# A two-layer hybrid decoder step on one core: three program blocks merged into one, with both layers written out

## The chip, the core and the metric

The kernel runs on one core of a Trainium2 chip. The metric is the device time of one execution in microseconds; the times below are the medians of several runs. A core has five engines that run side by side, each with its own stream of instructions: TensorE (PE, matrix products into PSUM), VectorE (DVE), ScalarE (ACT), GpSimd (POOL) and SyncE (SP), which here only issues transfers. They wait for each other by semaphores. A *block* of the program holds one stream for each engine. At the end of a block all engines meet at a barrier.

## What is computed

Two layers of a decoder on 512 prompt tokens and 8 sample tokens, width 1024, all in float32. The reference, cut to what matters here:

```python
def layer(x, pos, attn_fn, ctx_b, ctx_c, ctx_d, h0, p):
    u = rms_norm(x, p['g_pre_mix'])
    (q, k, v, qi, ki, wi, bx, gb, gc, glu, zg, xbc, dt) = jnp.split(u @ p['w_in'], cuts, axis=-1)
    ...                                   # sparse attention, two convolutions, a chunked state-space scan
    mix = jnp.concatenate([y_a, y_b, y_c, y_d], axis=-1) @ p['w_out']
    x = x + rms_norm(mix, p['g_post_mix'])
    hf = rms_norm(x, p['g_pre_ffn'])
    f = (jax.nn.silu(hf @ p['ffn_gate']) * (hf @ p['ffn_up'])) @ p['ffn_down']
    x = x + rms_norm(f, p['g_post_ffn'])
    return x, (k, v, ki, new_b, new_c, new_d, h_new.astype(x.dtype))

def rms_norm(x, g):
    xf = x.astype(jnp.float32)
    y = xf * lax.rsqrt(jnp.mean(xf * xf, axis=-1, keepdims=True) + RMS_EPS)
    return (y * g.astype(jnp.float32)).astype(x.dtype)
```

The outputs are the new activations of all tokens, and per layer the keys, values and states.

## The kernel before

**Data.** The activations `x` lie in SBUF with features on the partitions: 8 chunks `k` of 128 features by 520 tokens. Each float32 product is made of three: both operands are split into an *upper part* (ScalarE casts it, `*_hi`) and a *lower part* (value minus upper part, `*_lo`), and TensorE adds upper by upper, upper by lower and lower by upper. The lower part of a weight is made by GpSimd (lines 2474 and 2480) or VectorE (line 2120), that of an activation by VectorE (line 1704).

**Blocks.** There are three. The *prologue* (lines 351 to 412) loads the constants, the prompt (`x_rows`), and 24 small rows of parameters, turns `x` on TensorE (line 381), copies it out of PSUM (VectorE, line 408), squares it (ScalarE, line 400) and sums the squares over the features (TensorE, `sum_tokens`, line 335). The *layer* stands once, in a loop in hardware over both layers (line 554); weights are addressed by the loop's register. At its end come a barrier, the clearing of all the layer's semaphores, a barrier and the jump back. The *output* block turns `x` back (TensorE, line 2570), tile by tile of 128 tokens, copies it (VectorE, line 2579), and SP stores each tile of 128x1024 when both of its halves are there (line 2586).

**A layer's head.** SP issues seven transfers for the first three *slabs* of `w_in`, which give the outputs with tokens on the partitions: slab 0 in two pieces (`tw_raw`, and two small transfers for the `dt` columns into the same pieces), slab 1 in one, slab 2 in two. Then it stores `x` (`x_store`) and loads states and scalars. ScalarE takes the root of the mean square (`root_of`, line 1233), VectorE the reciprocal (line 1692), and TensorE spreads it over the partitions into PSUM (line 666). VectorE then scales the chunks (line 1700, one operand in SBUF, one in PSUM), ScalarE casts each (`u_hi`, line 1248), and VectorE subtracts (`m_lo`, line 1704); lower part k-2 follows scaling k. Between the casts of the chunks ScalarE casts the pieces of slab 0 (line 1241), ahead of chunks 1 and 3, and slab 1 after the last chunk; GpSimd makes their lower parts `tw_lo` (line 2480). TensorE's products with slab 0 (lines 742 to 744) wait for `tw_lo` and `m_lo`, chunk by chunk. After the first tile of slab 1 TensorE *turns* the indexer's queries and keys (line 710), which VectorE has rotated (`rope`, lines 1719 to 1760) behind them. The sparse attention and all else follow from there.

**A layer's end.** The last product with `ffn_down` (line 687) is squared and copied (ScalarE, lines 1661 and 1663), summed, rooted and spread as above. VectorE's `add_normed` scales each chunk (line 2228) and adds it to `x` (line 2232, two operands in SBUF). ScalarE squares the new chunk (line 1675) and TensorE sums (line 335), for the next layer's root; in the last layer this is done as well.

Of the kernel before, what the change touches and what calls it, by code (L numbers as in the profile page):

```python
# [26 lines left out]
ACT = mybir.ActivationFunctionType  # L27
# [90 lines left out]
def hybrid_decoder(nc, d, out):  # L118
# [16 lines left out]
    sems = []  # L135

    def sem(name):
        sems.append(ctx.enter_context(nc.semaphore(name)))
        return sems[-1]

    with ctx:
# [208 lines left out]
        with nc.Block() as block:  # L350
            @block.sync
            def _(sp):
                sp.dma_start(x8, d["x_sample"].rearrange("b s f -> (b s) f")).then_inc(sample_in, 16)
                sp.dma_start(cst[:, :], d["constants"]).then_inc(const_in, 16)
                for t in range(QT):
                    sp.dma_start(x_rows[:, t, :], d["x_prompt"][0, t * P:(t + 1) * P, :]).then_inc(rows_in, 16)
                sp.dma_start(pages[:, :], d["page_table"].rearrange("(o b) g -> o (b g)", o=1)).then_inc(pages_in, 16)
                for l in range(DEPTH):
                    for rows, tile in zip((ROWS_A, ROWS_B), rows_of[l]):
                        at = 0  # L360
                        for name, n in rows:
                            src = d[name][l:l + 1]
                            src = src.rearrange("o (c p) -> (o c) p", p=P) if src.ndim == 2 else \
                                src.rearrange("o t (c p) -> (o t c) p", p=P)
                            sp.dma_start(tile[at:at + n, :], src).then_inc(params_in, 16)
                            at += n
                sp.wait_ge(pages_in, 16)

            @block.tensor
            def _(pe):  # L370
                pe.wait_ge(const_in, 16)
                pe.wait_ge(sample_in, 16)
                for c in range(KC):
                    last = pe.transpose(bank(7)[:, c * NS:(c + 1) * NS], x8[:, c * P:(c + 1) * P], ident[0:NS, 0:NS])
                last.then_inc(x8_turned, 1)
                pe.wait_ge(rows_in, 16 * QT)
                for c in range(KC):
                    if c == 7:
                        pe.wait_ge(x_copied, 1)
                    for t in range(QT):  # L380
# [2238 lines left out]
```

## Time and profile before

| | us |
|---|---|
| median of 3 runs | 1496.69 |
| lowest and highest | 1494.46 and 1497.63 |
| the profiled execution | 1494.14 |
| its span, first to last instruction | 1492.6 |
| TensorE, products: busy | 1370.0 (92%), 11078 products |
| VectorE busy | 1029.2 (69%) |
| ScalarE busy | 654.5 (44%) |
| GpSimd busy | 195.8 (13%) |
| granted clock of TensorE, mean | 0.962 |

The span has three parts: the prologue to about 20 us, the two layers of about 732 us each, and the output from 1479.6 on. A row of the timeline gives the start and the length in us, the engine, the line of the kernel, the operation with what it writes and reads, how many instructions of the kind are merged into the row, and in brackets how long the engine was idle before and what released it. PEld is TensorE's load of weights, and SPq are transfers that SP issues. Rows of one engine may overlap by a tenth, since its instructions are pipelined.

### The profile page before, as it was taken

Reading aid. Unit: us, or ns where it says so; the run is one execution under the profiler, and the core shown is the slowest. Engines: PE = TensorE matmul, PEld = TensorE weight load, DVE = VectorE, ACT = ScalarE, POOL = GpSimd, SP = SyncE. Lnnn points to the kernel's source line nnn. Section 1 sums busy time; section 2 is a strip of 40 time slices with the busy share of each in tenths; the row PEclk is TensorE's granted clock in tenths of the full one; section 3 lists DMA queues with packets and bytes.
Section 4 is the critical chain, followed back from the end, with each engine's and each line's share of the span. In section 5 each row is a group of like instructions: output and inputs, shape, how many; then the busy total and the mean of one; then the engine's idle time right before and its main releaser. Section 6 shows DMA issues by size and latency. Waiting matters only on the chain. (4 is left out here: it accounts for less than half of the span.)

```text
span 1492.6 us, 29816 instructions
## 1 busy us (share of the span) xinstructions
PE 1370.0 (92%) x11078; PEld 1265.0 (85%) x11078; DVE 1029.2 (69%) x2147; ACT 654.5 (44%) x1199; POOL 195.8 (13%) x136
## 2 busy tenths in 40 slices
PE   4999978987999999999769998799979999999995
PEld 4889854787999999999657997648979999999994
DVE  5489998744899999322446898987269999972225
ACT  3443225443556666222344422445354566652222
POOL 1325312011000000010041442121100000000100
PEclk8999989998999999999879999999989999999997
DMA  6444231131523333432064333212322333343221
GB/s 222 137 119 115 72 100 60 62 99 43 156 72 110 101 99 103 155 96 89 9 209 141 110 85 89 68 63 84 96 92 86 100 101 110 100 142 112 88 67 58
DMA packets 223312, 149.96 MB, mean 100 GB/s; under 512 B 13579, under 2 KB 218739, under 8 KB 222167
## 3 DMA queue, kind: packets, MB, share of 16 engines
q1 hardware_dynamic: 220582, 141.09, 31.7%
q0 software_dynamic: 2624, 7.48, 1.3%
q8 instruction: 65, 1.06, 0.3%
q14 instruction: 41, 0.33, 0.1%
HBM read 128.92 MB, written 16.03 MB: 97 GB/s over the span
## 5 line engine op out<-in xcount | busy, mean ns | idle before, releaser
L1152 PE MATMUL PS<-b_hi,a_hi 128*128 128x260 f32 x1008 | 285.8, 284 | 3.0 <-DVE last_lo L2315 2.2
L1152 PE MATMUL PS<-b_lo,a_hi 128*128 128x260 f32 x1008 | 283.9, 282 | 0.0
L2120 DVE TENSOR_TENSOR w_lo<-ring,w_hi 128x640 fp32r<-128x640 f32 (+2 forms) x88 | 87.5, 994 | 242.3 <-ACT w_hi L1383 241.9
L1152 PEld LDWEIGHTS PS<-b_hi,a_hi 128*128 128x128 f32 x1008 | 189.6, 188 | 4.5 <-DVE last_lo L2315 2.7
L1152 PEld LDWEIGHTS PS<-b_lo,a_hi 128*128 128x128 f32 x1008 | 190.1, 189 | 0.0
L1383 ACT CAST w_hi<-ring 128x1024 fp32r<-128x1024 f32 (+2 forms) x92 | 80.1, 871 | 237.1 <-PE PS L687 237.1
L788 PE MATMUL PS<-u_hi,w_hi 128*128 128x260 f32 x576 | 122.1, 293 | 15.5 <-ACT hid L1325 15.5
L687 PE MATMUL PS<-hid_hi,w_lo 128*128 128x260 f32 x656 | 132.2, 283 | 0.0
L687 PE MATMUL PS<-hid_hi,w_hi 128*128 128x260 f32 x656 | 132.0, 282 | 0.0
L687 PE MATMUL PS<-hid_lo,w_hi 128*128 128x260 f32 x656 | 131.7, 282 | 0.0
L1152 PE MATMUL PS<-b_hi,s_lo 128*128 128x260 f32 x432 | 121.9, 282 | 0.0
L1152 PE MATMUL PS<-b_hi,raw_lo 128*128 128x260 f32 x432 | 121.9, 282 | 0.0
L2474 POOL TENSOR_TENSOR w_lo<-ring,w_hi 128x1024 fp32r<-128x1024 f32 x36 | 86.3, 2397 | 268.8 <-ACT w_hi L1271 268.8
L788 PE MATMUL PS<-m_lo,w_hi 128*128 128x260 f32 x576 | 120.7, 289 | 0.0
L788 PE MATMUL PS<-u_hi,w_lo 128*128 128x260 f32 x576 | 120.1, 289 | 0.0
L788 PEld LDWEIGHTS PS<-u_hi,w_hi 128*128 128x128 f32 x576 | 90.9, 192 | 22.3 <-ACT hid L1325 16.9
L2544 POOL TENSOR_TENSOR side<-side 128x520 f32<-128x520 f32 x12 | 15.7, 1310 | 709.9 <-ACT u L1663 709.9
L687 PEld LDWEIGHTS PS<-hid_hi,w_lo 128*128 128x128 f32 x656 | 101.0, 188 | 0.0
L687 PEld LDWEIGHTS PS<-hid_hi,w_hi 128*128 128x128 f32 x656 | 101.0, 188 | 0.0
L687 PEld LDWEIGHTS PS<-hid_lo,w_hi 128*128 128x128 f32 x656 | 101.0, 188 | 0.0
L1555 ACT CAST a_hi<-ring 128x512 fp32r<-128x512 f32 x144 | 89.5, 622 | 16.5 <-PE PS L1152 16.2
L788 PEld LDWEIGHTS PS<-m_lo,w_hi 128*128 128x128 f32 x576 | 91.1, 192 | 2.9 <-issue 2.9
(396 smaller groups left out, 3351.7 us busy)
## 6 DMA issues: line engine op xcount, KB each, us to landing
ring<-in_ffn_gate SPq DMA_DIRECT2D x44, 512.0 KB, 3.6
ring<-in_ffn_up SPq DMA_DIRECT2D x44, 512.0 KB, 3.7
ring<-in_w_in SPq DMA_DIRECT2D x36, 512.0 KB, 3.7
ring<-in_ffn_down SPq DMA_DIRECT2D x32, 384.0 KB, 3.4
ring<-in_ffn_down SPq DMA_DIRECT2D x32, 320.0 KB, 3.1
x_store<-x SPq DMA_DIRECT2D x4, 2080.0 KB
x<-x_store SPq DMA_DIRECT2D x4, 2080.0 KB, 7.8
ring<-in_w_out SPq DMA_DIRECT2D x16, 512.0 KB, 4.1
```

The lines of the kernel that those rows point to most:

```text
L687: ins = pe.matmul(to[:, h, :], w[:, k - base, :], a[k][:, h * HALF:(h + 1) * HALF], start=(begin and w is whi and a is a_hi), stop=(end an ...
L788: last = pe.matmul(bank(tile_bank(i) + h)[:, 0:HALF], w[i % 2][:, k, :], t[:, h * HALF:(h + 1) * HALF], start=(k == 0 and a == 0), stop=(k ...
L1152: ins = pe.matmul(bank(ACC[up][to])[:, 0:HALF], w[:, k, :], b[:, k, :], start=(start and k == 0 and w is whi and b is bhi), stop=(k == KC ...
L1383: act.copy(w_hi[part % 2][:, 0:n, :], raw[part % 4][:, 0:n, :]).then_inc(part_hi, 1)
L1555: act.copy(a_hi[hi_block(q, at)][:, :, :], source if q not in (S1, S2, S4) else source[:, :, :])\
L2120: dve.tensor_tensor(w_lo[part % 2][:, 0:n, :], raw[part % 4][:, 0:n, :], w_hi[part % 2][:, 0:n, :].bitcast(F32), ALU.subtract).then_inc(pa ...
L2474: pool.tensor_tensor(w_lo[f % 2][:, :, :], raw[(f + 2) % 4], w_hi[f % 2][:, :, :].bitcast(F32), ALU.subtract).then_inc(tile_lo, 1)
L2544: pool.tensor_tensor(squares[:, 0, :], squares[:, 0, :], squares[:, m, :], ALU.add).then_inc(added, 1)
```

## The change

The three blocks become one, and the barriers and the clearing of semaphores between them go. The loop over the layers is written out when the program is built: `layer` is a number, and the code of a layer stands twice. A semaphore is not cleared any more; each has a count of what one layer adds to it (`sem(name, in_layer)`), and `past(layer, s, value)` adds the earlier layers' part to what is waited for. All waits inside a layer are rewritten so; of these the diff shows two. Waits and addresses inside the remaining inner loops still go by registers.

With the fences gone, five things move:

- SP asks for layer 0's slabs behind the prologue's small loads, and for layer 1's slabs when the last product of layer 0 is done (`down_part`). `x_store` waits for `x`.
- ScalarE casts the two pieces of slab 0 ahead of all chunks: in layer 0 right behind the root, in layer 1 already at the end of layer 0, ahead of squares 2 and 4. Their lower parts stay on GpSimd.
- The last layer's squares and their sum go.
- TensorE turns the output chunk by chunk of features: after each chunk's add the four tiles' piece, in two halves of four chunks. The small tile of the samples is turned at the end of each half.
- The copies out of PSUM go from VectorE to ScalarE, and SP stores each half of a tile (128x512) as it is copied.

```diff
-        sems = []
-        def sem(name):
-            sems.append(ctx.enter_context(nc.semaphore(name)))
-            return sems[-1]
+        per_layer = {}
+        def sem(name, in_layer=0):
+            s = ctx.enter_context(nc.semaphore(name))
+            per_layer[s.num] = in_layer
+            return s
...
+        def past(l, s, value):
+            return s, value + l * per_layer[s.num]
...
-        with nc.Fori(0, DEPTH) as layer:
-            with nc.Block() as block:
-                @block.sync
-                def _(sp):
+                for layer in range(DEPTH):
                     l = layer
...
+                    if layer:
+                        sp.wait_ge(*past(layer, down_part, 0))
                     for (a, b, _, _), t in zip(tok_pieces[0], slab_raw[0]):
...
+                    if layer:
+                        sp.wait_ge(*past(layer, x_updated, 0))
+                    else:
+                        sp.wait_ge(x_copied, KC + 1)
                     sp.dma_start(x_store, x[:, :, :].rearrange("p k t -> p (k t)")).then_inc(x_kept, 16)
...
+                for n, (t, q) in enumerate(Y_ORDER):
+                    sp.wait_ge(*past(DEPTH, y_copied, n + 1))
+                    to = y_prompt[0, t * P:(t + 1) * P, :] if t < QT else y_sample.rearrange("b s f -> (b s) f")
+                    sp.dma_start(to[:, q * 512:(q + 1) * 512], y_rows[0:P if t < QT else NS, t, q * 512:(q + 1) * 512])\
+                      .then_inc(y_stored, 16)
...
-                    sum_squares(pair(0), squares_ready, KC)
+                    if layer + 1 < DEPTH:
+                        sum_squares(pair(0), squares_ready, KC)
+                for q in range(2):
+                    for c in range(4):
+                        pe.wait_ge(*past(DEPTH, x_updated, 4 * q + c + 1 - KC))
+                        for t in range(QT):
+                            if q == 1 and c == 0 and t >= 2:
+                                pe.wait_ge(*past(DEPTH, y_copied, t - 1))
+                            last = pe.transpose(bank(Y_BANK[t, q])[:, c * P:(c + 1) * P], x[:, 4 * q + c, t * P:(t + 1) * P], ident)
...
                     root_of(0, pair(0), 1.0 / D_MODEL, 0)
+                    if layer == 0:
+                        slab_upper(0, 0)
+                        slab_upper(0, 1)
                     for k in range(KC):
-                        if k in (1, 3):
-                            slab_upper(0, k // 2)
-                        act.wait_ge(m_scaled_ready, k + 1)
+                        act.wait_ge(*past(layer, m_scaled_ready, k + 1))
...
-                    for k in range(KC):
-                        act.wait_ge(x_updated, KC + k + 1)
+                    for k in range(KC if layer + 1 < DEPTH else 0):
+                        if k in (2, 4):
+                            slab_upper(0, k // 2 - 1, layer + 1)
+                        act.wait_ge(*past(layer, x_updated, KC + k + 1))
                         act.activation(squares[:, k, :], x[:, k, :], ACT.Square).then_inc(squares_ready, 1)
+                for n, (t, q) in enumerate(Y_ORDER):
+                    m = P if t < QT else NS
+                    act.wait_ge(*past(DEPTH, y_turned, n + 1))
+                    act.copy(y_rows[0:m, t, 512 * q:512 * (q + 1)], bank(Y_BANK[t, q])[0:m, :]).then_inc(y_copied, 1)
...
-            nc.all_engine_barrier()
-            nc.gpsimd.sem_clear(range(sems[first_layer_sem].num, sems[last_layer_sem - 1].num + 1))
-            nc.all_engine_barrier()
```

How the instructions stand, at three places. A row gives the line, the operation, what it writes and reads, the size, and the semaphores that it waits for.

SP between the prologue and layer 0, before. `arena<-in_dconv_b` is the last small load, `tw_raw` are the slabs' pieces:

```order
L365 DMA arena<-in_dconv_b 6x128
L350 UNCONDITIONAL_BRANCH [waits pages_in]
L554 UNCONDITIONAL_BRANCH [waits barrier_Pool_Activation_PE_DVE_SP_release]
L557 UNCONDITIONAL_BRANCH
L565 ISA
L565 DMA tw_raw_75<-in_w_in 128x4x4
```

And now, without a fence between them:

```order
L514 DMA arena<-in_dconv_b 6x128
L526 DMA tw_raw_75<-in_w_in 128x4x4 [waits pages_in]
L526 DMA tw_raw_76<-in_w_in 128x4x4
L529 DMA tw_raw_75<-in_w_in 128x4x296
L529 DMA tw_raw_76<-in_w_in 128x4x296
L529 DMA tw_raw_79<-in_w_in 128x8x384
L529 DMA tw_raw_84<-in_w_in 128x3x384
L529 DMA tw_raw_85<-in_w_in 128x5x384
L534 DMA x_store<-x 128x4160 [waits x_copied]
```

The slabs' transfers moved up to the small loads, in the same order, and `x_store` waits for `x`.

ScalarE at the end of a layer, before. `side` and `u` take the last product, `arena<-x` are the eight squares:

```order
L1661 ACTIVATE side<-PS 128x520 [waits down_part]
L1663 COPY u<-PS 128x520
L1233 ACT_TABLE_LOAD
L1233 ACTIVATE root<-PS,cst 128x130 [waits sums_ready]
L1675 ACTIVATE arena<-x 128x520 [waits x_updated] x8
L555 UNCONDITIONAL_BRANCH
L554 REGISTER_ALU [waits barrier_Pool_Activation_PE_DVE_SP_release]
L554 COMPARE_AND_BRANCH
```

And now, from the end of layer 0 into layer 1:

```order
L1248 ACT_TABLE_LOAD
L1248 ACTIVATE root<-PS,cst 128x130 [waits sums_ready]
L1693 ACTIVATE arena<-x 128x520 [waits x_updated] x2
L1256 CAST tw_hi_71<-tw_raw_75 128x1200 [waits slab_in00,dt_w_in]
L1693 ACTIVATE arena<-x 128x520 [waits x_updated] x2
L1256 CAST tw_hi_72<-tw_raw_76 128x1200 [waits slab_in01,dt_w_in]
L1693 ACTIVATE arena<-x 128x520 [waits x_updated] x4
L1248 ACTIVATE root<-PS,cst 128x130 [waits sums_ready]
L1264 CAST u_hi<-arena 128x520 [waits m_scaled_ready] x8
L1256 CAST tw_hi_77<-tw_raw_79 128x3072 [waits slab_in10]
```

The two casts of slab 0 stand between the squares, and the next layer's root follows the last square with no table load. The chunks' eight casts stand in one piece, and slab 1's cast is behind them as before.

TensorE at the end of the program, before. `arena` are the squares and `cst,x` the transposes; `turned_ready` counts the copies of the output:

```order
L335 MATMUL PS<-arena,cst 32x130 [waits squares_ready]
L335 MATMUL PS<-arena,cst 32x130 x3
L555 UNCONDITIONAL_BRANCH
L554 REGISTER_ALU [waits barrier_Pool_Activation_PE_DVE_SP_release]
L554 COMPARE_AND_BRANCH
L2561 UNCONDITIONAL_BRANCH
L2570 MATMUL PS<-cst,x 128x128 x32
L2570 MATMUL PS<-cst,x 8x128 [waits turned_ready]
L2570 MATMUL PS<-cst,x 8x128 x3
```

And now, the last two chunks of the first half, and the first of the second:

```order
L1229 MATMUL PS<-cst,x 128x128 [waits x_updated]
L1229 MATMUL PS<-cst,x 128x128 x3
L1229 MATMUL PS<-cst,x 128x128 [waits x_updated]
L1229 MATMUL PS<-cst,x 128x128 x3
L1234 MATMUL PS<-cst,x 8x128 [waits turned_ready]
L1234 MATMUL PS<-cst,x 8x128 x3
L1229 MATMUL PS<-cst,x 128x128 [waits x_updated]
L1229 MATMUL PS<-cst,x 128x128
L1229 MATMUL PS<-cst,x 128x128 [waits turned_ready] x2
```

The transposes now stand right behind the last spread; each group of four waits for one add of `x`, and only the second half's first chunk and the small tiles wait for copies too.

## Rows read from the trace of the kernel before

**Rows 1.** The page, costliest groups: busy, mean | idle before, what ended it

```profile
L1152 PE MATMUL PS<-b_hi,a_hi 128*128 128x260 f32 x1008 | 285.8, 284 | 3.0 <-DVE last_lo L2315 2.2
```

**Rows 2.** Timeline, prologue to layer 0: start, length, engine, line, operation, count [idle before]

```profile
12.24 0.30 SPq L365 DMA_DIRECT2D arena<-in_dconv_b  x1
...
17.07 1.83 ACT L400 ACTIVATE u<-x 128x520 f32<-128x520 f32 x3 [0.20 <-DVE x L408]
...
17.79 1.98 PE L335 MATMUL PS<-u,cst 128*32 128x130 f32 x64
...
20.80 1.28 ACT L1233 ACT_TABLE_LOAD   x1 [1.90 <-PEq L414]
...
20.95 1.02 SPq L565 DMA_DIRECT2D tw_raw<-in_w_in  x2
...
22.09 0.37 ACT L1233 ACTIVATE root<-PS,cst 128x130 f32<-128x130 f32 x1
...
25.65 2.09 DVE L1700 SCALAR_TENSOR_TENSOR arena<-x,par,PS 128x520 f32<-128x520 f32 x3 [2.19 <-PE PS L666]
```

**Rows 3.** Timeline, head of layer 0

```profile
26.97 1.19 ACT L1241 CAST tw_hi<-tw_raw 128x1200 fp32r<-128x1200 f32 x1
...
28.24 5.90 POOL L2480 TENSOR_TENSOR tw_lo<-tw_raw,tw_hi 128x1200 fp32r<-128x1200 f32 x2 [27.53 <-ACT tw_hi L1241]
...
28.93 2.59 DVE L1704 TENSOR_TENSOR m_lo<-arena,u_hi 128x520 fp32r<-128x520 f32 x1
...
31.11 0.59 PE L742 MATMUL PS<-tw_hi,u_hi 128*128 128x300 f32 x1 [5.50 <-POOL tw_lo L2480]
...
38.48 2.77 ACT L1241 CAST tw_hi<-tw_raw 128x3072 fp32r<-128x3072 f32 x1
...
41.32 13.93 POOL L2480 TENSOR_TENSOR tw_lo<-tw_raw,tw_hi 128x3072 fp32r<-128x3072 f32 x3 [7.18 <-ACT tw_hi L1241]
...
57.20 1.53 PE L710 MATMUL PS<-cst,arena 128*128 128x128 f32 x12 [0.99 <-DVE arena L1760]
...
57.89 1.56 ACT L1265 COPY arena<-PS 128x512 f32<-128x512 f32 x3 [1.10 <-PE PS L710]
```

**Rows 4.** Timeline, end of layer 0 to the turn in layer 1

```profile
730.27 0.41 PE L687 MATMUL PS<-hid_hi,w_lo 128*128 128x260 f32 x2
...
739.15 0.64 ACT L1675 ACTIVATE arena<-x 128x520 f32<-128x520 f32 x1 [0.64 <-DVE x L2232]
...
740.97 0.69 DVE L2232 TENSOR_TENSOR x<-x,u 128x520 f32<-128x520 f32 x1
...
744.80 1.31 DVE L2232 TENSOR_TENSOR x<-x,u 128x520 f32<-128x520 f32 x2
...
746.22 1.27 PE L335 MATMUL PS<-arena,cst 128*32 128x130 f32 x16 [0.62 <-ACT arena L1675]
...
752.96 1.94 SPq L565 DMA_DIRECT2D tw_raw<-in_w_in  x2
...
757.93 2.09 DVE L1700 SCALAR_TENSOR_TENSOR arena<-x,par,PS 128x520 f32<-128x520 f32 x3 [2.19 <-PE PS L666]
...
789.48 1.53 PE L710 MATMUL PS<-cst,arena 128*128 128x128 f32 x12 [1.77 <-DVE arena L1760]
```

**Rows 5.** Stretches: us, busy time and count of each engine, granted clock, DMA

```profile
733.00:736.00 3.00, 1.16 (x8) 0.97 (x8) 1.16 (x2) 0.47 (x2) 0.00 (x0) 1.00 0.00 0
...
738.00:747.50 9.50, 5.23 (x64) 1.61 (x64) 8.11 (x13) 4.94 (x8) 0.00 (x0) 0.50 0.01 2
...
755.00:758.00 3.00, 2.10 (x8) 1.80 (x8) 0.81 (x2) 0.00 (x0) 0.00 (x0) 0.50 0.67 152
```

**Rows 6.** Timeline, end of the run

```profile
1476.88 1.30 DVE L2232 TENSOR_TENSOR x<-x,u 128x520 f32<-128x520 f32 x2
...
1481.58 7.35 PE L2570 MATMUL PS<-cst,x 128*128 128x128 f32 x40 [2.02 <-PEq L2555]
...
1486.99 3.14 DVE L2579 COPY arena<-PS 128x512 f32<-128x512 f32 x5 [0.16 <-PE PS L2570]
```

More of the change, by code:

```diff
@@ L1230, in root_of, with _ @@
+            @block.scalar
+            def _(act):
+                for k in range(KC):
+                    act.wait_ge(x_copied, k + 2)
+                    act.activation(x_squares[:, k, :], x[:, k, :], ACT.Square).then_inc(x_squared, 1)
+                for layer in range(DEPTH):
                     def root_of(n, sums, scale, eps):
-                        if n:
-                            act.wait_ge(sums_ready, n)
+                        if n or layer:
+                            act.wait_ge(*past(layer, sums_ready, n))
+                        else:
+                            act.wait_ge(x_summed, 1)
@@ L1378, in upper @@
                     def upper(part, free, value, turn, n=KC):
-                        act.wait_ge(raw_in[part % 4], turn)
-                        act.wait_ge(free, value)
+                        act.wait_ge(*past(layer, raw_in[part % 4], turn))
+                        act.wait_ge(*past(layer, free, value))
                         act.copy(w_hi[part % 2][:, 0:n, :], raw[part % 4][:, 0:n, :]).then_inc(part_hi, 1)
@@ L2458, in _ @@
                         lower(p, 4 * KC - 8 + DN0 + p + 1, DOWN_PARTS[p % 4][1])
-                    dve.wait_ge(down_ready, 2 * KC + 4)
+                    dve.wait_ge(*past(layer, down_ready, 2 * KC + 4))
                     add_normed(3, u, "g_post_ffn")
-                    dve.wait_ge(x_updated, 2 * KC)
-                @block.gpsimd
-                def _(pool):
+                    dve.wait_ge(*past(layer, x_updated, 2 * KC))
+            @block.gpsimd
+            def _(pool):
+                for layer in range(DEPTH):
                     l = layer
@@ L2477, in slab_lower @@
                     def slab_lower(s, i):
-                        pool.wait_ge(slab_hi, sum(len(p) for p in tok_pieces[:s]) + i + 1)
+                        pool.wait_ge(*past(layer, slab_hi, sum(len(p) for p in tok_pieces[:s]) + i + 1))
                         pool.tensor_tensor(tw_lo[s][i][:, :, :], slab_raw[s][i][:, :, :], tw_hi[s][i][:, :, :].bitcast(F32),
```

878 lines of the change are left out of this document (424 added, 454 removed).

## The prediction

> **What bounds the kernel now.** I read the page first, then the timeline at the three places where one block of the program ends and the next begins, because that is where the diff acts. In the page's groups the long stretches belong to TensorE: the largest matmul group has 3.0 us of idle time in 285.8 us of work [rows 1]. The diff leaves these stretches alone. At the three fences TensorE waits instead, and a chain that hops between engines sets the time. At the first one the last square sum ends at 19.77, and ScalarE's root starts at 22.09, behind a barrier and a table load of 1.28 us [rows 2]. At the one between the layers the sum ends at 747.49, and the first weight transfer is issued at 752.96 [rows 4]. At the last one ScalarE and TensorE finish a sum of squares that nobody reads, and the transposes for the output start at 1481.58 [rows 6].
>
> The reader should also see who holds whom in a layer's head. GpSimd's two lower parts take 5.90 us together, and during them VectorE's lower parts of the activations take 2.59 us where the same size takes 0.69 (0.69 is the add's row) [rows 3, 4]. TensorE starts at 31.11, when the first lower part is there. A second chain runs beside it: the last activation, then the cast of slab 1 at 38.48, GpSimd's three lower parts to 55.25, VectorE's rope step behind them, and TensorE's turn at 57.20, which waits 0.99 us for it [rows 3]. So the head has two paths that end within 1 us of each other.
>
> **The change, part by part.** All sums are against the profiled execution: span 1492.6, run 1494.14.
>
> *Prologue to layer 0.* The weights' seven transfers are issued once the small loads are out, near 12.7 instead of 20.95 (the last small load is issued at 12.24) [rows 2]. In the run before, the first cast was not held up at 26.97, 6.0 us after the first issue [rows 2, 3], so they are there by 18.7. ScalarE's squares end at 18.90 [rows 2]; the table load still stands ahead of the root, so the root runs at about 20.2, 1.85 earlier. The root to the first scaled chunk took 3.56 us [rows 2], with the spread at the slow clock: 2.10 us of TensorE at 0.50 against 1.16 at 1.00 [rows 5]. Here TensorE has rested only 1.9 us, so I take the fast one: 20.2 + 3.56 - 0.94, some 23.0 after rounding up (bounds 22.8 and 23.8). That is 2.6 earlier than 25.65. The casts follow the root at once (2 x 1.19), so GpSimd works from 21.9 to 27.8 (5.90) [rows 3]. VectorE's first lower part comes up at 25.1, three scalings later (2.09), and is held to about 28.2. TensorE starts there instead of at 31.11: 2.9 us. Only one lower part is held now instead of two, 2.5 us lost instead of 3.8, so the second chain gains 2.6 + 1.3 = 3.9. At the turn the first path gains 2.9 and the 0.99 of waiting that goes, also 3.9. **Layer 0: 3.9 us** (bounds 2.9, if only TensorE's start counts, and 5.6, if VectorE slips in between GpSimd's two operations).
>
> *Layer 0 to layer 1.* The barriers, the clearing of semaphores and the jump back go, and ScalarE's table load with them, since the root's function set is already in place. If that were all, the root would come at 747.6, 0.1 after the sum. But the first slab's casts are now placed between the squares, after the second and the fourth. Their weights can be asked for from 730.68 on, when the last product ends [rows 4]; by the 6.0 us above they are there by 737. The first cast starts at 739.8, right behind the second square, and the second at 742.3. ScalarE has the room: a square takes 0.64 in a step of 1.28 [rows 4]. GpSimd then runs from 741.0 to 746.9, and VectorE's adds of two SBUF operands, 0.69 each, fall under it. The add at 740.97 gets in, just; the next waits to 744.0 and the one after to 746.9, and each ends 0.4 later, as the held rows did. The last two follow behind two scalings, and the last add ends near 749.3 instead of 746.11 [rows 4]: 3.2 us back. (If GpSimd wins the tie at 740.97, it is 3.9.) From the last add to the end of the sum is 1.38 (746.11 to 747.49), so the root runs at 750.7, and 3.56 later, at 754.3, the first chunk is scaled; TensorE's clock is at 0.50 in such a stretch of thin sums [rows 5], so I take the slow spread. That is 3.6 before 757.93. From there on no lower part is held: 3.8 more for the second chain, 7.4 in all. The first path would be 6.4 earlier and loses its 1.77 of waiting at 789.48 [rows 4], 8.2, so the second chain decides. **Layer 1: 7.4 us** (bounds 5.5, with a further add held, and 10.6, with none).
>
> The Trainium skill ("SBUF — State Buffer", section "SBUF: two separate sides") says that GpSimd and a VectorE operation with two SBUF inputs take one port pair as an exclusive lock for the whole instruction. By that rule the scalings, which read one operand from PSUM, go free, and the adds do not; the row of 2.59 us agrees [rows 3].
>
> *The end.* The squares and the sum of the last layer go. TensorE's 32 large transposes, 7.35 us with the small ones [rows 6], are done chunk by chunk as the adds end. An add comes each 1.28 us and four transposes take at most 0.92 (7.35 over eight chunks), so all but the last chunk is hidden. After the last add, 1478.18 [rows 6], the first tile's bank is complete at about 1478.75. The copies move to ScalarE: 0.52 each for 128x512 from PSUM [rows 3], four of them and the samples' small one, to about 1481.4. Before, the last copy ended at 1490.13 and the span 2.47 later [rows 6]. I keep the 2.47, since the last large transfer is half the size. **End: 8.8 us** (bounds 7.5, if each copy takes 0.69 as VectorE's did and the queue adds to the tail, and 9.3).
>
> *With one answer each:* constants instead of registers in waits, and fixed addresses in transfers, touch sequencers that wait anyway: nothing. x's store in layer 1 stands behind the weights on SP's queue and waits for the last add; what is behind it (the states, the caches) stood behind the weights before too, is issued earlier now, and is wanted only at the turn or later. GpSimd's waits for the stores at a layer's end now stand ahead of its first lower part, and those stores are long out.
>
> Sum: 3.9 + 7.4 + 8.8 = 20.1. The span would be 1472.5, the profiled run 1474.0, and against the median, which is 2.55 above the profiled run, **1476.6**.
>
> **The rivals.**
> *A: the adds are not held.* For it: none of the trace's adds ever met GpSimd, so their rows all read 0.69. Against: the lower parts have the same operand form and were held. Layer 1 gains 10.6 instead of 7.4: 1473.4.
> *B: smaller gains all along.* The transfers of 4.3 MB now run beside the prologue's loads, so the casts come late and layer 0 gains 2; two further waits at the layers' fence leave 4.7; the end gives 7.5. Together 14.2: 1482.5. For it: no row shows these transfers beside other loads. Against: they have 7.9 us until the first cast (12.7 to 20.6) where 6.0 was enough, and the pieces needed first are first in the queue.
> *C: it does nothing.* The head's gain is used up by a later wait on VectorE's top-k chain, and the end waits on the output transfers, 2 MB. Against: both paths that leave the head shift together, and the output transfers kept up before. Within 3 us of 1496.7.
> *D: slower, by fetching code.* With the layers written out the program is twice as long, and the loops that remain sit at other addresses. A taken jump may have to fetch its target: the fence with the jump back took 5.5 us (747.49 to 752.96) [rows 4], the last one without it left TensorE idle for 2.0 [rows 6], so 3.5 us for a jump is the bound. TensorE jumps back 16 times in the program's inner loops (6 and 2 in each layer): 56 us, 1532.6. It decides from 6 such jumps on. Against: the same loops with the same bodies show no gap now [rows 1].
> The Trainium skill ("Runtime: NRT & Kernel Launch", section "Instruction fetch mechanics") says that a taken branch to a target outside the current window stalls for a fetch. No row separates this from the barrier; it speaks for a gain at the fence as much as for D.
>
> **How the numbers follow.** Forecast 0.60, its own range 1474.5 to 1480; A 0.13; B 0.17; C 0.03; D 0.04; the rest, between B and C, 0.03. The range 1470.5 to 1482 takes in the forecast and its bounds (some 24 to 16 us of gain, and 1 us for the medians' scatter), A, and a third of B: about 0.8. A measurement of this kernel can tell about 0.2%, 3 us, from no change. Faster by more: 0.93, within: 0.03, slower: 0.04.
>
> **What the profile after would show.** TensorE's first slab product at about 28.2; the cast of slab 1 near 34.6; no table load before the second root. At the layers' fence one or two adds of 2 to 3 us beside GpSimd, the last one ending near 749.3 less the 3.9 of layer 0, and then the root within 1.5 us. In layer 1 all lower parts at 0.69. At the end the transposes between the adds, and some 5.7 us from the last add to the end of the span. Wrong would be: adds all at 0.69 (A), casts waiting on transfers (B), or gaps in TensorE at a loop's first product (D).

## The result, and the profile after

The changed kernel takes 1477.53 us (median of 4 runs, 1474.74 to 1478.38), the kernel before 1495.58 on the same chip (4 runs, 1490.53 to 1497.63). The ratio is 0.988, with a 95% interval of 0.985 to 0.991: 18.05 us or 1.2% faster. In a later series of five runs it was 1474.72 against 1493.17, ratio 0.988 again (0.986 to 0.990). The profiled execution took 1478.38 with a span of 1476.4 us; before it was 1494.14 and 1492.6.

The sum can be read at a few marks that both programs have. The first is the end of the prologue's last square sum. Then come TensorE's transposes behind VectorE's rope step in each layer (the "turn"), the first add of the expert output to x in each layer, and the start of the row with the last two adds. All columns are profiled executions; "again" is a second one, of the later series.

| stretch | before | after | again | gain of after | of again |
|---|---|---|---|---|---|
| start to the last square sum | 19.77 | 19.26 | 20.81 | 0.5 | -1.0 |
| sum to the turn of layer 0 (head) | 37.43 | 33.44 | 33.74 | **4.0** | **3.7** |
| turn to the first add (nothing changed in it) | 679.94 | 681.15 | 678.69 | -1.2 | 1.25 |
| first add to the turn of layer 1 (fence and head) | 52.34 | 45.84 | 45.73 | **6.5** | **6.6** |
| turn to the last two adds (nothing changed in it) | 687.40 | 688.76 | 688.78 | -1.4 | -1.4 |
| last two adds to the end | 15.72 | 7.95 | 7.95 | **7.8** | **7.8** |
| span | 1492.6 | 1476.4 | 1475.7 | 16.2 | 16.9 |

The three edited places give 18.3 and 18.1 us, which is what the medians say. What the profiled spans lack of it was lost in the start and in stretches that the edit does not touch.

The timeline of after, from the prologue into layer 0, answers [rows 2, 3]. As there, a row gives start and length in us, engine, line, operation, what it writes and reads, the count, and in brackets the idle time before and its releaser:

```profile
12.07 0.95 SPq L526 DMA_DIRECT2D tw_raw<-in_w_in  x2
...
18.62 1.28 ACT L1248 ACT_TABLE_LOAD   x1
...
19.91 0.37 ACT L1248 ACTIVATE root<-PS,cst 128x130 f32<-128x130 f32 x1
...
20.18 2.27 ACT L1256 CAST tw_hi<-tw_raw 128x1200 fp32r<-128x1200 f32 x2
21.44 5.40 POOL L2513 TENSOR_TENSOR tw_lo<-tw_raw,tw_hi 128x1200 fp32r<-128x1200 f32 x2 [20.98 <-ACT tw_hi L1256]
23.14 2.09 DVE L1732 SCALAR_TENSOR_TENSOR arena<-x,par,PS 128x520 f32<-128x520 f32 x3 [1.86 <-PE PS L661]
...
25.14 2.25 DVE L1736 TENSOR_TENSOR m_lo<-arena,u_hi 128x520 fp32r<-128x520 f32 x1
...
27.45 0.62 PE L737 MATMUL PS<-tw_hi,u_hi 128*128 128x300 f32 x1 [4.35 <-DVE m_lo L1736]
...
33.74 2.76 ACT L1256 CAST tw_hi<-tw_raw 128x3072 fp32r<-128x3072 f32 x1
...
36.58 13.83 POOL L2513 TENSOR_TENSOR tw_lo<-tw_raw,tw_hi 128x3072 fp32r<-128x3072 f32 x3 [9.74 <-ACT tw_hi L1256]
...
52.70 1.53 PE L705 MATMUL PS<-cst,arena 128*128 128x128 f32 x12 [0.61 <-DVE arena L1792]
```

The casts run straight behind the root, without waiting for a transfer. One lower part of VectorE meets GpSimd and takes 2.25 us, the others 0.69. TensorE starts at 27.45 instead of 31.11, and its wait at the turn is 0.61 instead of 0.99.

The same program between the layers, answering [rows 4]:

```profile
733.85 0.70 DVE L2264 TENSOR_TENSOR x<-x,u 128x520 f32<-128x520 f32 x1
...
736.39 1.18 ACT L1256 CAST tw_hi<-tw_raw 128x1200 fp32r<-128x1200 f32 x1
...
737.74 6.36 POOL L2513 TENSOR_TENSOR tw_lo<-tw_raw,tw_hi 128x1200 fp32r<-128x1200 f32 x2 [23.20 <-ACT tw_hi L1256]
...
738.96 2.56 DVE L2264 TENSOR_TENSOR x<-x,u 128x520 f32<-128x520 f32 x1
...
742.11 2.55 DVE L2264 TENSOR_TENSOR x<-x,u 128x520 f32<-128x520 f32 x1
...
745.25 1.30 DVE L2264 TENSOR_TENSOR x<-x,u 128x520 f32<-128x520 f32 x2
...
747.99 0.37 ACT L1248 ACTIVATE root<-PS,cst 128x130 f32<-128x130 f32 x1 [0.78 <-PE PS L337]
...
751.56 2.09 DVE L1732 SCALAR_TENSOR_TENSOR arena<-x,par,PS 128x520 f32<-128x520 f32 x3 [2.20 <-PE PS L661]
...
779.69 1.53 PE L705 MATMUL PS<-cst,arena 128*128 128x128 f32 x12 [0.61 <-DVE arena L1792]
```

The root follows the last add by 1.44 us and has no table load ahead of it. But two of the eight adds take 2.56 and 2.55 us beside GpSimd's first pair of lower parts. The first add in the timeline of before:

```profile
737.14 0.69 DVE L2232 TENSOR_TENSOR x<-x,u 128x520 f32<-128x520 f32 x1
```

Now it comes 3.29 us earlier, and the last one ends 0.44 later (746.55 against 746.11 [rows 4]): 3.73 us given back.

The end, answering [rows 6]:

```profile
1465.37 1.12 PE L1229 MATMUL PS<-cst,x 128*128 128x128 f32 x4 [0.16 <-DVE x L2264]
1465.89 2.05 ACT L1697 COPY arena<-PS 128x512 f32<-128x512 f32 x4 [9.02 <-PE PS L1229]
...
1467.50 1.02 PE L1234 MATMUL PS<-cst,x 128*8 128x128 f32 x4 [1.01 <-ACT arena L1697]
...
1468.32 3.62 PE L1229 MATMUL PS<-cst,x 128*128 128x128 f32 x16
1468.45 1.31 DVE L2264 TENSOR_TENSOR x<-x,u 128x520 f32<-128x520 f32 x2
...
1471.33 2.48 ACT L1697 COPY arena<-PS 128x512 f32<-128x512 f32 x5 [2.20 <-PE PS L1229]
```

The transposes now stand between the adds, four of them (1.12 us) per chunk. From the end of the last add (1469.76) to the end of the span are 6.6 us; before they were 14.4.

### The profile page after: what moved, and what is told of

Its sections match the earlier page's. It is cut to its first block, busy times and chain, and to the rows that moved or that the text cites. A ratio compares the mean times of both kernels' runs of the same rounds, so it can differ in the third digit from the quotient of the medians.

```text
span 1476.4 us, 29324 instructions
## 1 busy us (share of the span) xinstructions
PE 1370.9 (93%) x11014; PEld 1269.0 (86%) x11014; DVE 1018.2 (69%) x2137; ACT 653.4 (44%) x1200; POOL 195.5 (13%) x136
## 4 chain that ended last, share of the span: by engine, by line
PE 82%; DVE 12%; ACT 3%; issue 2%; DMA 1%; SPq 0%; ACTq 0%; DVEq 0%
PE PS L682 30%; PE PS L1147 24%; PE PS L783 12%; PE PS L754 2%; PE PS L910 2%; PE PS L755 2%; PE PS L756 2%; PE PS L661 1%; DVE x L2264 1%; PE PS L698 1%; PE PS L737 1%; PE PS L738 1%; PE PS L739 1%; PE PS L337 1%; DVE arena L1751 1%
## 5 line engine op out<-in xcount | busy, mean ns | idle before, releaser
L783 PEld LDWEIGHTS PS<-u_hi,w_hi 128*128 128x128 f32 x576 | 91.6, 194 | 22.4 <-ACT hid L1341 16.9
L1571 ACT CAST a_hi<-ring 128x512 fp32r<-128x512 f32 x144 | 89.5, 621 | 16.5 <-PE PS L1147 16.2
```

Of the source, the lines that this page charges most:

```text
L783: last = pe.matmul(bank(tile_bank(i) + h)[:, 0:HALF], w[i % 2][:, k, :], t[:, h * HALF:(h + 1) * HALF], start=(k == 0 and a == 0), stop=(k ...
L1571: act.copy(a_hi[hi_block(q, at)][:, :, :], source if q not in (S1, S2, S4) else source[:, :, :])\
```

## The experiments

Two series were run, each on one chip beside the kernel before (median 1493.51 of 7 runs in the first, 1493.17 of 8 in the second). The names in brackets are the labels of the table behind them.

**Is the give-back between the layers GpSimd holding VectorE's adds (e1)?** Layer 1's first casts move behind the second root, as layer 0 has them, so that GpSimd starts when the adds are over:

```
-                    if layer == 0:
-                        slab_upper(0, 0)
-                        slab_upper(0, 1)
+                    slab_upper(0, 0)
+                    slab_upper(0, 1)
...
-                        if k in (2, 4):
-                            slab_upper(0, k // 2 - 1, layer + 1)
```

> Edit: layer 1's two casts of slab 0 stand behind the second root, as in layer 0, and no longer between the squares; the weights are still asked for early. Theory (port lock): GpSimd is then idle under layer 0's adds, so all eight take 0.69 us and the last one ends 3.7 us sooner after the first (9.0 instead of 12.7). In layer 1 GpSimd's two operations hold one activation lower part for 2.3 us, as in layer 0 of the changed kernel, and from the first scaled chunk to the turn it takes 29.5 instead of 28.2 us. Net 2.3 us faster than the changed kernel. Rival (the early casts pay): slab 0 is then what TensorE waits for, and the head of layer 1 loses the 3.8 us that were forecast for it: as fast as the changed kernel or up to 1.5 us slower.

Timeline of this kernel, between the layers:

```profile
738.70 1.30 DVE L2261 TENSOR_TENSOR x<-x,u 128x520 f32<-128x520 f32 x2
...
741.72 2.27 ACT L1256 CAST tw_hi<-tw_raw 128x1200 fp32r<-128x1200 f32 x2
...
743.07 5.41 POOL L2510 TENSOR_TENSOR tw_lo<-tw_raw,tw_hi 128x1200 fp32r<-128x1200 f32 x2 [31.03 <-ACT tw_hi L1256]
...
747.03 2.01 DVE L1733 TENSOR_TENSOR m_lo<-arena,u_hi 128x520 fp32r<-128x520 f32 x1
```

The adds are free of delay again: from the start of the first (731.04) to the end of the last are 8.96 us, as before the change (8.97), where after has 12.70. One lower part of the activations is held in their place (2.01). From the first add to the turn are 43.57 us, 2.3 less than in after. Five profiles with after's code at this place read 45.7 to 46.4, so the difference is real and 2.2 to 2.9 in size. The adds were held by GpSimd, and casting between the squares costs more than it brings.

**What if GpSimd has no lower part there at all (e2)?** In layer 1 VectorE makes slab 0's two lower parts itself, in the gaps on both sides of its reciprocal:

```
+                        if layer:
+                            slab0_lower(0)
...
+                        if layer:
+                            slab0_lower(1)
...
-                    for s in range(N_TOK):
+                    for s in range(1 if layer else 0, N_TOK):
```

> Edit: in layer 1 VectorE makes slab 0's two lower parts, the first between the last add and the reciprocal (it is idle there for 1.85 us), the second between the reciprocal and the first scaling (idle 2.2 us); layer 0 and the casts are as in the changed kernel. Theory (port lock): the adds are free, 3.7 us sooner, and each lower part, some 1.4 us by VectorE's 1.23 us for 1024 columns, lies in a gap, so that nothing is given back: 3.7 us faster than the changed kernel at the turn of layer 1. Rival (the adds are late for another reason, such as ScalarE's casts between the squares): the adds still take 2.6 us twice, and the two lower parts change nothing or cost up to 2.8 us.

Timeline of this kernel, VectorE between the last add and the first lower part of the activations:

```profile
743.79 1.40 DVE L1729 TENSOR_TENSOR tw_lo<-tw_raw,tw_hi 128x1200 fp32r<-128x1200 f32 x1
...
745.33 0.97 DVE L1724 RECIPROCAL rstd<-root 128x130 f32<-128x130 f32 x1
746.21 1.34 DVE L1729 TENSOR_TENSOR tw_lo<-tw_raw,tw_hi 128x1200 fp32r<-128x1200 f32 x1
...
750.50 0.69 DVE L1746 TENSOR_TENSOR m_lo<-arena,u_hi 128x520 fp32r<-128x520 f32 x1
```

VectorE needs 1.40 and 1.34 us for what took GpSimd about 3 us each, and it has this time: nothing waits for it there. First add to turn 42.28, 3.6 us less than in the profile of after (3.4 to 4.2 over the five). The 3.73 us given back are regained.

**What did the fence cost, the meeting of the engines or what came with it (e4)?** The engines meet between the layers by a semaphore, and layer 1's weights are asked for and cast behind it; no jump, no clearing, no table load:

```
+                    if layer:
+                        sp.sem_inc(x8_turned, 1)
+                        sp.wait_ge(x8_turned, 6)
...
```

The same stands in each engine's program at the layer's start, and the casts stand as in e1.

> Edit: between the layers all five engines meet at a semaphore again; weights are asked for and cast behind it; no jump back, no clearing of semaphores, no table load. All else as in the changed kernel. Theory (the jump, the clearing and the table load are the price of the fence, the meeting itself costs some 0.3 us): from the end of the last sum to the issue of the first weight transfer 0.5 instead of 5.5 us, adds free (3.7 us less than the changed kernel), root at once, but the casts wait for the weights, 6 us after the issue, and two lower parts are held again; from the first scaled chunk to the turn about 32 us. So within 1.5 us of the changed kernel at the turn. Rival (the meeting itself costs, or the early request is what pays): 4 us or more slower than the changed kernel at the turn.

Timeline of this kernel, the last square sum, the first request and the root:

```profile
740.71 1.27 PE L337 MATMUL PS<-arena,cst 128*32 128x130 f32 x16 [0.62 <-ACT arena L1699]
...
741.42 0.94 SPq L529 DMA_DIRECT2D tw_raw<-in_w_in  x2
...
742.11 0.37 ACT L1257 ACTIVATE root<-PS,cst 128x130 f32<-128x130 f32 x1 [0.84 <-PE PS L337]
```

The last square sum ends at 741.98 and the root runs at 742.11; SP had issued the weights at 741.42, ahead of the sum's modelled end. In the kernel before 5.47 us lay between the sum and this issue [rows 4]. From the first add to the turn are 46.6 us, 5.8 less than before and within 0.9 of after's five profiles. So this meeting is cheap. It is also a weak one, as it let the engines go before TensorE's last products had ended; whether a block's barrier waits for them is not known. What was dear is that wait, the clearing, the jump back or the start of each engine's program anew, and this run does not tell these apart. In the changed kernel the weights' early request brings almost nothing at this place, because its gain goes into the held adds. Without that it pays: e1 and e4 both cast behind the root, and e1, which asks early and has no meeting, is 3.0 us faster to the turn (43.57 against 46.58).

**Is it the early request in layer 0 (e5)?** SP asks for the weights of layer 0 only when the first square sum is there, about where the kernel before did:

```
+                    else:
+                        sp.wait_ge(x_summed, 1)
```

> Layer 0's weights are asked for only when the first square sum is done, about where the kernel of before asked for them; everything else as in the changed kernel. Theory, that in layer 0 the earlier request carries the gain: casts from about 25.4 us instead of 20.2, the first slab product at 32 to 33 us instead of 27.45, the turn of the first slab about 5 us later than 52.7, and the time about as much longer than the changed kernel's. Rival, that the chain of root, reciprocal and scalings sets the start and the weights would be early enough anyway: the turn at most 1 us later.

Timeline of this kernel, the first cast of slab 0:

```profile
25.03 1.19 ACT L1258 CAST tw_hi<-tw_raw 128x1200 fp32r<-128x1200 f32 x1 [4.47 <-DMA tw_raw<-in_w_in]
```

The casts come at 25.03 and wait for the transfer, and from the sum to the turn are 37.15 us, against 33.44 in after and 37.43 before. So nearly the whole gain in layer 0 is the early request; without it the missing barrier is worth only 0.3 us. TensorE's first slab product came at 29.64, earlier than I expected, because VectorE's first lower part got in between GpSimd's two (1.19 us), and only the second was held in full (2.58). So the turn is 3.7 us late and not 5.

**How much of the end is the order of the output (e3)?** The blocks are merged, but the output is made as before: the square sum is kept, transposes stand behind it, VectorE copies, and each tile is sent whole.

> Edit: the output as in the kernel before (squares and sum of the last layer kept, transposes tile by tile behind them, copies by VectorE, whole rows stored), but in the same block without a fence. All else as in the changed kernel. Theory (the chunk by chunk order is worth its share, the fence 2 us): from the last add to the end of the span 12.4 us (14.4 before, less the 2.0 us fence), so 5.8 us slower than the changed kernel, which took 6.6. Rival (most of the tail was the fence, and the end is set by the transfers): 9 us or less, 2.4 us slower at most.

Timeline of this kernel, its end:

```profile
1467.49 5.77 PE L1229 MATMUL PS<-cst,x 128*128 128x128 f32 x40
1468.72 6.39 DVE L2489 COPY arena<-PS 128x512 f32<-128x512 f32 x10 [2.69 <-PE PS L1229]
```

The transposes start 0.1 us after the sum (1467.41) instead of 2.0 after it [rows 6]. From the last add (1466.03) to the end are 11.4 us: 3.0 of the 7.8 us come with the missing block border, 4.8 with the new order. The border's share is more than its 2.0 us of waiting, since the 40 transposes also took 5.77 us instead of 7.35: TensorE's granted clock was 0.50 from 1467 to 1469, 0.76 to 1471 and 1.00 behind that, and before it was 0.50 from 1481 to 1487.

**What holds the new end (e6)?** The samples' transposes shared a PSUM bank with a tile's; now that tile has a free bank, and VectorE copies two of the second halves beside ScalarE:

```
-        Y_BANK = {(0, 0): 0, (1, 0): 1, (2, 0): 2, (3, 0): 3, (4, 0): 2, (0, 1): 6, (1, 1): 7, (2, 1): 0, (3, 1): 1, (4, 1): 3}
+        Y_BANK = {(0, 0): 0, (1, 0): 1, (2, 0): 2, (3, 0): 3, (4, 0): 6, (0, 1): 7, (1, 1): 0, (2, 1): 1, (3, 1): 2, (4, 1): 3}
...
+                for t in (1, 3):
+                    dve.wait_ge(*past(DEPTH, y_turned, QT + 1 + t + 1))
+                    dve.tensor_copy(y_rows[0:P, t, 512:1024], bank(Y_BANK[t, 1])).then_inc(params_turned, 1)
```

> Only the end is changed: tile 4's first half has a bank of its own, so that its transposes wait for no copy, and the second halves of tiles 1 and 3 are copied by VectorE beside ScalarE. Theory, that the end of the changed kernel is set by the five copies of 0.5 us in a row on ScalarE and by the transposes that start 1.1 us behind the last add: last add to the end of the span 5.2 us instead of 6.64, the time 1.4 us shorter than the changed kernel's. Rival, that the last transfer's own time sets it: 6.3 to 6.6 us.

Timeline of this kernel, its end:

```profile
1464.21 1.27 PE L1232 MATMUL PS<-cst,x 128*128 128x128 f32 x8 [0.23 <-DVE x L2270]
1465.18 1.53 ACT L1703 COPY arena<-PS 128x512 f32<-128x512 f32 x3 [1.81 <-PE PS L1232]
...
1465.36 1.29 DVE L2502 COPY arena<-PS 128x512 f32<-128x512 f32 x2 [0.60 <-PE PS L1232]
```

Last add (1464.76) to the end of the span: 5.5 us instead of 6.6. The first copy of a second half starts 0.42 us behind the last add instead of 1.57; this is the whole gain, and sharing the copies brought nothing on top. (The last transposes also ran at a granted clock of 1.00 here, at 0.50 in after. For the first copy that is worth 0.1 us at most, as only one of them stands ahead of it behind the last add.) The rate of the transfers says why. First after, from 1460 to 1477 in 40 slices of 0.425 us, then this kernel, from 1455 to 1471 in slices of 0.4:

```profile
GB/s 0 0 0 0 0 0 0 0 0 0 0 0 0 0 0 0 0 260 405 410 415 390 405 222 0 0 0 0 0 0 337 405 424 400 390 414 135 0 0 0
```

```profile
GB/s 0 0 0 0 0 0 0 0 0 0 0 0 0 0 0 0 0 0 220 404 410 405 410 400 399 16 0 0 0 338 405 410 389 410 405 307 0 0 0 0
```

The second burst is near 400 GB/s in both, in after from about 1472.8 to 1475.7, in this kernel from 1466.6 to 1469.4. Each starts 0.9 us after the first copy's end, and ends 0.7 to 0.9 before the span does. A second half of 1.05 MB takes 2.6 us at that rate. So both my copies and the rival's transfer were half right: the first copy starts the end, and the stream of transfers sets its length. The median of all runs, 1474.84, does not show the 1.1 us beside 1474.72, as the scatter of single runs is larger (1471.33 to 1478.07).

**Both together (e7), and the changed kernel again (e0).** VectorE makes slab 0's lower parts in both layers, with the end of e6:

> VectorE makes slab 0's lower parts in both layers (in layer 0 the first behind the reciprocal and the second behind the last scaling), and the output copies are shared as in the kernel with the end alone changed. Theory, that GpSimd's two-operand subtractions hold VectorE's wherever they meet: against the changed kernel the head of layer 0 loses the held scaling's 1.5 us, the stretch from the first expert add of layer 0 to the turn of layer 1's first slab falls from 45.85 to 42.2 us, and the end from 6.6 to 5.2: the span 6.6 us shorter than the changed kernel's. Rival, that VectorE's own work in those gaps delays its squares and scalings as much as it saves: layer 0's head gains nothing or loses up to 1 us, and the whole is 4 to 5 us faster, nearly all of it from the fence and the end.

> The changed kernel itself once more, beside the kernel of before and the other kernels of this call, so that they can be compared on one chip. Both readings (the clock granted between 300 and 372 us and between 800 and 1140 us was chance, or it belongs to the changed kernel) are told apart here: by the first the gain at the turn of layer 0 (4.5 us) still stands to within 0.5 us at the last product of layer 0 in at least one of the two profiles of this kernel, by the second both profiles show it falling to 3.6 us.

The marks of all profiled executions, in us; the ratios are each to the kernel before in the same series (after's own: 1495.58; e1 to e4: 1493.51), and "unchanged" is a stretch that no edit touches:

| kernel | sum to turn, layer 0 | unchanged | first add to turn, layer 1 | unchanged | last add to the end | median us (runs) | ratio to before |
|---|---|---|---|---|---|---|---|
| before | 37.43 | 679.94 | 52.34 | 687.40 | 14.4 | 1493.17 (8) | |
| after | 33.44 | 681.15 | 45.84 | 688.76 | 6.6 | 1477.53 (4) | 0.988 |
| after again, e0 | 33.74 | 678.69 | 45.73 | 688.78 | 6.6 | 1474.72 (5) | 0.988 |
| e1, casts late | 33.51 | 679.10 | 43.57 | 684.59 | 6.6 | 1473.72 (4) | 0.987 |
| e2, VectorE's lower parts in layer 1 | 33.56 | 681.13 | 42.28 | 684.45 | 6.7 | 1470.36 (4) | 0.985 |
| e3, old output | 33.61 | 676.92 | 46.29 | 688.09 | 11.4 | 1481.33 (4) | 0.992 |
| e4, meeting kept | 33.67 | 677.73 | 46.58 | 688.70 | 6.7 | 1476.73 (4) | 0.988 |
| e5, asked late | 37.15 | 679.16 | 46.38 | 686.28 | 6.7 | 1478.93 (4) | 0.991 |
| e6, end | 33.62 | 676.81 | 46.44 | 686.31 | 5.5 | 1474.84 (4) | 0.988 |
| e7, VectorE's in both layers, end of e6 | 32.67 | 678.61 | 42.15 | 689.14 | 5.5 | 1468.64 (5) | 0.983 |

The last kernel beats both: 0.983 of before, with an interval of 0.981 to 0.985, and 6.1 us below the changed kernel by the medians of one series. By the marks it is 0.8 to 1.1 in layer 0, 3.6 to 3.7 in layer 1 and 1.1 at the end. In layer 0 the theory wanted 1.5, and its rival nothing or a loss. The missing part seems to have another cause. From the timelines, first e0, then e7, the spread of the reciprocals ahead of the scalings:

```profile
22.52 1.16 PE L661 MATMUL PS<-rstd,cst 128*128 128x130 f32 x8 [1.71 <-DVE rstd L1724]
```

```profile
21.66 1.84 PE L664 MATMUL PS<-rstd,cst 128*128 128x130 f32 x8 [2.12 <-DVE rstd L1730]
```

The spread takes 2.10 us at half the clock and 1.16 at the full one [rows 5]; it read 1.16 in five of the nine profiles and 1.23 to 1.84 in the others, with the same code. In e7 it took 0.68 us more than in e0; the granted clock from 21.5 to 23.6 was 0.73 and then 0.50 there, and 1.00 in e0. From the last sum to the first slab product are 6.76 us in e7 and 7.83 in e0; this 1.07 is also the gain at the turn. With the spread of e0 it would be 1.75 by my estimate; no run shows it. That the turn follows TensorE's start is new, too: in both kernels GpSimd now waits 0.75 us for slab 1's second cast, which stands behind ScalarE's copy of TensorE's products. Timeline of e7, GpSimd in layer 0:

```profile
35.43 6.80 POOL L2533 TENSOR_TENSOR tw_lo<-tw_raw,tw_hi 128x3072 fp32r<-128x3072 f32 x1 [34.97 <-ACT tw_hi L1260]
42.98 6.94 POOL L2533 TENSOR_TENSOR tw_lo<-tw_raw,tw_hi 128x1152 fp32r<-128x1152 f32 x2 [0.75 <-ACT tw_hi L1260]
```

So the two chains out of a layer's head are level, and a gain on one of them alone is soon worth nothing. The same fits the 45.7 to 46.4 that this code's stretch read in layer 1. From the first slab product to ScalarE's first copy were 14.4 to 14.5 us where it was shortest (after, e0) and 14.9 to 15.1 where GpSimd had to wait 0.6 to 0.8 (e3, e5, e6).

The columns "unchanged" show what the 2.6 us are that the profile of after lost there (1.2 and 1.4). The second profile of the changed kernel does not fall back in layer 0: it gains 1.25 us there where the first lost 1.2. The stretch takes 676.8 to 681.2 us, the other 684.5 to 689.1. Their means over the nine profiles of changed programs are 678.8 and 687.2, against 679.9 and 687.4 in the one profile of before. TensorE's clock is part of that scatter. From the views by stretches (length, then busy time and count of each engine, granted clock, DMA share, GB/s), the first row of before, the second of after, the third of e6:

```profile
300.00:372.00 72.00, 60.59 (x511) 58.20 (x508) 31.44 (x46) 29.97 (x45) 11.44 (x8) 0.93 0.22 65
```

```profile
300.00:372.00 72.00, 61.40 (x493) 59.06 (x491) 30.75 (x43) 31.47 (x47) 11.45 (x8) 0.88 0.18 54
```

```profile
300.00:372.00 72.00, 60.85 (x523) 57.72 (x525) 32.19 (x42) 32.42 (x50) 11.43 (x8) 0.93 0.18 54
```

At a mean of 0.88 TensorE is busy 61.40 us of these 72, at 0.93 it is 60.85. Which of the two comes does not follow the edit: before, e1, e3, e4, e5 and e6 show 0.93; after, e0, e2 and e7 show 0.88. It does not explain all of the scatter (e7 has 0.88 and a short stretch), and the rest I leave open.

## Why the prediction was right

The forecast was 1476.6 us and the median is 1477.53; the range and the sign held. The gain itself was put at 20.1 and is 18.05 (medians) or 18.0 to 18.3 (marks), so the sum was a tenth too large. The time came out closer than that because the kernel before also measured 1.1 us lower once its fourth run was in (1495.58 instead of 1496.69).

*Layer 0, forecast 3.9, measured 4.0 and 3.7.* The mechanism held: transfers issued at 12.07, the root at 19.91 (20.2 expected) with the casts straight behind it, first scaling at 23.14 (23.0), one lower part held, first product at 27.45 (28.2), slab 1's cast at 33.74 (34.6). The late request (e5) shows that the gain is the transfer's place in SP's queue. That the sum came out to 0.1 us is in part luck, since errors of its terms cancel. Measured from the last square sum, the first scaling is only 2.0 us earlier (3.88 behind it instead of 5.88), where I had 2.6: the root came 0.3 early, less than the 0.5 by which the prologue was shorter by chance, and the spread took 1.76 us and not 1.16, at a granted clock of 0.61 and then 0.50. The other term, forecast at 1.3, is 2.2: from the first scaling to GpSimd's work on slab 1 are 13.44 us instead of 15.67, because the held lower part took 2.25 and not 3.1. It ends with GpSimd's pair, which started 0.46 before my 21.9 and took 5.40 instead of 5.90. In e0, with the fast spread, the terms were 3.0 and 1.6, and GpSimd then waited 0.75 for a cast. TensorE's wait at the turn did not go either; it is 0.61 instead of 0.99.

*Layers' fence and head, forecast 7.4, measured 6.5 (5.9 to 6.6 over the five profiles with this code).* The mechanism was the forecast's and not rival A's: no table load, root 1.44 us behind the last add, all lower parts of the activations at 0.69, and two adds held. Even the tie went as said: with all times of the forecast 3.3 earlier, as the first add came, the first cast (739.8) lies at 736.5 and was at 736.39, and the add at 740.97 lies at 737.67, where it got in 0.06 us ahead of GpSimd. The mis-sized term is what follows: I had 3.2 us and it was 3.73. I had let GpSimd take 5.90 us, as in layer 0 before, where one operation of VectorE got in ahead of its second lower part. Here the add that got in holds GpSimd's first one as well, and the pair took 6.36, 0.46 more; both held adds wait for it.

Another 0.34 is in the rope step. Before, VectorE's first operation got in ahead of GpSimd and the second was held (timeline, VectorE in layer 0):

```profile
50.54 0.52 DVE L1719 TENSOR_TENSOR arena<-arena,cst 128x256 f32<-128x256 f32 x1 [10.61 <-ACT arena L1287]
50.98 4.41 DVE L1720 TENSOR_TENSOR arena<-arena,cst 128x128 f32<-128x128 f32 x1
55.31 0.28 DVE L1721 TENSOR_TENSOR arena<-arena,cst 128x128 f32<-128x128 f32 x1
```

After, it is the first one that is held, so one more has to follow when GpSimd is done:

```profile
46.43 4.27 DVE L1751 TENSOR_TENSOR arena<-arena,cst 128x256 f32<-128x256 f32 x1 [11.24 <-ACT arena L1303]
50.62 0.28 DVE L1752 TENSOR_TENSOR arena<-arena,cst 128x128 f32<-128x128 f32 x1
50.82 0.28 DVE L1753 TENSOR_TENSOR arena<-arena,cst 128x128 f32<-128x128 f32 x1
```

From GpSimd's last lower part to the turn are 2.29 us now and 1.95 before (55.25 to 57.20), in both layers. The prediction moved this chain as a rigid whole. In layer 0 the forecast came out in spite of it, as slab 1's cast was early.

*End, forecast 8.8, measured 7.8.* The step that failed is the one that had the first tile's last bank complete 0.57 us after the last add; it was 1.57. The samples' transposes at 1467.50 waited 1.01 us for ScalarE to copy a bank which they share, and they stand in TensorE's order ahead of the second half's. Two chunks whose adds were done at 1466.60 and 1467.88 waited behind them, so 16 transposes of 0.23 us were still to do at 1468.32. With a bank of its own (e6) the first copy of the second half starts 0.42 us after the last add. The copies (2.48 us for five) and the time behind the last one (2.59 against 2.47) were right.

*The unchanged stretches* were put at nothing. Over many profiles that is right to about 1 us, in a single one a layer's stretch lay up to 3.1 us from its reading before.

*The range.* I gave its bounds as some 24 to 16 us of gain. Those of the three parts add up to 25.5 (5.6, 10.6 and 9.3) and 15.9; nothing in the result hangs on it.

*The rivals.* A fell: two adds held in after, and in e0, e3, e5 and e6 as well. B's condition fell: the casts waited for nothing. C fell with the gain of 18 us. D fell: the largest matmul group has 3.0 us idle as before, and the stretches that hold the inner loops took no longer than before (means of 678.8 and 687.2 us against 679.9 and 687.4). From the page of after (busy, mean | idle before, what ended it):

```profile
L1147 PE MATMUL PS<-b_hi,a_hi 128*128 128x260 f32 x1008 | 286.2, 284 | 3.0 <-DVE last_lo L2347 2.2
```

The Trainium skill says ("Runtime: NRT & Kernel Launch", section "Instruction fetch mechanics") that a taken branch out of the window stalls for a fetch. The trace bears out no such price for the inner loops. For the jump back between the layers e4 agrees in direction: without it 5.5 us shrink to nearly nothing, though clearing and restarting went with it.

## What to carry to other kernels

When a fence goes, look for what the engines behind it will now do at the same time. Here more than a third of what the fence gave between the layers went into GpSimd running beside VectorE's adds, and moving two small steps from GpSimd to an idle gap of VectorE brought it back. A transfer's place in its queue can be worth more than the barrier that one removes: in layer 0 the early request was nearly the whole gain. And with single profiles 4 to 5 us apart in stretches that no edit touches, count an edit of a few us between marks on both sides of it, not from the spans.

## What the runs showed of the hardware

A VectorE operation of two SBUF operands is held for as long as GpSimd's own runs: an add of 0.69 us took 2.56 and 2.55, a lower part of the activations 2.25, a rope step of 0.28 took 4.41. The scaling with one operand in PSUM kept its 0.75 between them. It works in both directions. One of GpSimd's lower parts of 128x1200 took 2.72 us where no such operation was ahead of it and 3.18 to 3.23 where one had just got in. So the pair took 5.40 us with none ahead (layer 0 of after), 5.90 with one, which slipped in between the two (layer 0 before), and 6.36 with one ahead of each (between the layers of after). This is the exclusive port pair that the Trainium skill describes ("SBUF — State Buffer", section "SBUF: two separate sides"), and the numbers agree. What I had not expected is how much hangs on the order of arrival: 0.46 us between the layers, 0.34 in the rope step.

With a meeting of five engines over a semaphore (e4) the root ran 0.13 us behind the sum, without one (after) 0.07; a block border with clearing, jump and table load put it 6.9 us behind (747.49 [rows 4] to 754.37).

The transfers of 1.05 MB at the end ran near 400 GB/s and started 0.9 us after the end of the first copy that they waited for.
